# Router logits from the unnormalised rows, an early choice for four tiles, block counts by shift and scan, and a last down product that reads its weights in the ring

## What is computed

```python
def hier_moe(xn, w_rg, b_rg, w_re, b_re, w1, w3, w2):   # xn = rmsnorm(x2) * ffn_norm_g
    lg = xt @ w_rg + b_rg                  # 4 groups, top 1
    le = (xt @ w_re + b_re)[chosen group]  # 8 experts in it, top 2
    gate = pg_top * pe_top / sum(pe_top)
    # rows of one expert lie together, block after block
    ...
    h = silu(xb @ w1[e]) * (xb @ w3[e])    # 1024 -> 512
    y = (h @ w2[e]) * gate                 # 512 -> 1024
    out[token] += y
# then out + x2, and a last rmsnorm with final_norm_g
```

## Time and profile before

| | |
|---|---|
| median of 3 runs | 1295.69 us |
| the profiled execution's own time | 1297.7 us |
| its span, first to last instruction | 1295.9 us |
| mean granted TensorE clock | 0.933 of full speed |
| busy: PE, DVE, ACT, POOL | 1136.1, 516.1, 421.7, 253.7 us |
| weight loads of the experts | 96 of 2048 KB |
| DMA moved | 299.47 MB |

### The profile page before, as it was taken

The page is one execution under the profiler, slowest core; times in us unless marked ns, Lnnn a source line. Parts: engine busy times, 40 slices in busy tenths (PEclk is TensorE's granted clock), DMA queues, the critical chain, the costliest instruction groups (busy, mean ns, idle before and its releaser), DMA issues.

```text
span 1295.9 us, 15806 instructions
## 1 busy us (share of the span) xinstructions
PE 1136.1 (88%) x5178; PEld 699.2 (54%) x5178; DVE 516.1 (40%) x881; ACT 421.7 (33%) x668; POOL 253.7 (20%) x276
## 2 busy tenths in 40 slices
PE   2999999999988977999984899989999879899960
PEld 1788888888856645888873333333333223333320
DVE  3541111112337756755445334433424333424117
ACT  4422222223146555533214124232423332424222
POOL 0011111111107001000000234423434223424220
PEclk9999999999989966999995899989999899999985
DMA  7153331711160001742379399999989999999506
GB/s 292 58 187 114 114 112 50 267 57 49 49 244 1 1 1 52 241 130 87 114 285 415 145 363 393 421 419 419 405 353 378 421 420 419 420 416 405 228 24 279
DMA packets 66591, 299.47 MB, mean 231 GB/s; under 512 B 8672, under 2 KB 8800, under 8 KB 41216
## 3 DMA queue, kind: packets, MB, share of 16 engines
q1 hardware_dynamic: 53488, 264.44, 51.5%
q0 software_dynamic: 13072, 34.63, 6.8%
HBM read 272.29 MB, written 35.91 MB: 238 GB/s over the span
## 4 chain that ended last, share of the span: by engine, by line
PE 62%; DMA 18%; DVE 7%; issue 5%; ACT 5%; SPq 1%; DVEq 0%; ACTq 0%; POOLq 0%; POOL 0%
DMA rawe<-in_w 16%; PE ps L535 12%; PE ps L536 12%; PE ps L537 12%; PE ps L818 11%; PE ps L839 4%; ACT cur L1142 3%; PE ps L634 2%; PE ps L655 2%; PE ps L667 1%; PE ps L808 1%; PE ps L646 1%; PE ps L752 1%; DVE cur13b L1578 1%; DVE att L1291 1%
## 5 line engine op out<-in xcount | busy, mean ns | idle before, releaser
L818 PE MATMUL ps<-cur13a,xT 128*64 128x512 f32 x656 | 163.3, 642 | 37.2 <-DVEq L1580 36.4
L535 PE MATMUL ps<-whi,xTh 128*128 128x512 f32 x480 | 188.2, 392 | 6.2 <-DVE xTl L1228 4.1
L536 PE MATMUL ps<-wlo,xTh 128*128 128x512 f32 x480 | 187.7, 391 | 0.0
L537 PE MATMUL ps<-whi,xTl 128*128 128x512 f32 x480 | 187.6, 391 | 0.0
L839 PE MATMUL ps<-cur,hT 128*64 128x512 f32 x656 | 152.5, 607 | 4.3 <-ACTq L1145 4.3
L1173 DVE TENSOR_TENSOR wlo<-raw,whi 128x2048 fp32r<-128x2048 f32 x27 | 61.7, 2291 | 218.2 <-ACT whi L862 218.0
L818 PE MATMUL ps<-cur13b,xT 128*64 128x512 f32 x656 | 148.6, 592 | 0.0
L1556 DVE COPY xT<-ps 128x512 f32<-128x512 f32 x41 | 28.4, 691 | 296.3 <-PE ps L808 296.3
L818 PEld LDWEIGHTS ps<-cur13a,xT 128*64 128x64 f32 x656 | 53.1, 146 | 118.3 <-issue 116.0
L913 ACT ACTIVATE zst<-ps 128x512 f32<-128x512 f32 x60 | 35.9, 600 | 235.1 <-PE ps L537 235.1
L1142 ACT ACTIVATE cur<-rawe 128x4096 f32 x31 | 112.2, 3620 | 0.1
(11 more groups left out here) (216 smaller groups left out, 1477.3 us busy)
## 6 DMA issues: line engine op xcount, KB each, us to landing
rawe<-in_w SPq DMA_DIRECT2D x96, 2048.0 KB, 17.6
raw<-in_w_in SPq DMA_DIRECT2D x20, 1024.0 KB, 5.8
z_scratch<-zst POOLq DMA_DIRECT2D x60, 256.0 KB, 2.3
gat<-z_scratch SPq DMA_DIRECT2D x12, 512.0 KB, 3.9
xn_scratch<-rrow POOLq DMA_DIRECT2D x6, 1024.0 KB, 4.5
ya<-y_scratch SPq DMA_DIRECT2D x6, 1024.0 KB, 9.9
raw<-in_w_out SPq DMA_DIRECT2D x4, 1024.0 KB, 8.0
xin<-in_x_prompt SPq DMA_DIRECT2D x4, 512.0 KB, 7.8
```

The costliest lines, as they stand in the source:

```text
L535: pe.matmul(out, ah, bh, start=first, stop=False)
L536: pe.matmul(out, ah, bl, start=False, stop=False)
L537: return pe.matmul(out, al, bh, start=False, stop=last)
L818: mm = pe.matmul(ps[0][u * CAP:(u + 1) * CAP, :], xT[:, c, h * CAP:(h + 1) * CAP], cur13[h][:, :, c * 512 + u * 256:c * 512 + u * 256 + 25 ...
```

## The change

1. PE's router columns come from `x2` and no longer from `rrow`, so they wait for `s_x2`. The gain is multiplied into the router weights once, on POOL (a new small load `gcol` on SP, a new semaphore `s_wrg`), and the row's root multiplies the logits in `route_logits`.
2. The logits of tile t-1 stand behind the first quarter of tile t's second half instead of behind the half.
3. `choose` runs for tiles 0 to 3 while the last tile is projected, and for tiles 4 and 5 at the end. PE makes the ranks in two parts to match (`count`): the first ahead of the last tile's logits, the second behind them.
4. The block counts come from a shift by 6 bits and one scan over the 32 experts, instead of the threshold table and five doubling steps. The two picks lie in one tile `A12`, so that one product and one sum serve both. The four steps on the block's expert stand behind the sixth pair of one-hot tables, and PE's product of them behind its ninth table product.
5. POOL's first two gathers take their index straight from `idxt`, and POOL reads the count of blocks behind the first gather instead of ahead of it.
6. The last `down` reads w2 in the ring (`rawe`) and waits for the loads, not for ACT's copy.
7. In the projection's tiles the root takes nine steps (`rsqrt_column`), the first of which nothing waits for. The last norm keeps eleven.

The diff, cut to its core (tile addresses, names of constants and unchanged code that only moved are left out):

```diff
+    A12 = at("A12", D_O + 768, [P, 2, NT, NE])
...
+    wide = at("wide", D_O + 7 * KB, [P, NE])
+    wint = at("wint", D_O + 7 * KB + 128, [P, NE], U32)
+    ends = at("ends", D_O + 7 * KB + 256, [P, NE])
+    zero = at("zero", D_O + 7 * KB + 384, [P, NE])
...
+            sp.dma_start(gcol[:, :], A["ffn_norm_g"][0].rearrange("(p c) -> p c", c=KC)).then_inc(s_rp, 16)
...
-                pe.wait_ge(s_rr, t + 1)
+                pe.wait_ge(s_x2, 2 * t + 2)
...
-                        mm = pe.transpose(ps[j][:, c * P:(c + 1) * P], rrow[t % 2][:, 4 * j + c::KC], ident)
+                        mm = pe.transpose(ps[j][:, c * P:(c + 1) * P], x2[:, t, 4 * j + c::KC], ident)
...
-                    pe.wait_ge(s_rp, 16 * 3)
+                    pe.wait_ge(s_wrg, 1)
...
+                        if t >= 1 and n == 1 and j == 0:
+                            logits(t - 1)
                     mm.then_inc(s_w, 1)
                     if t >= 1 and n == 0:
                         route_columns(t - 1)
-                if t >= 1:
-                    logits(t - 1)
             route_columns(NT - 1)
...
+            def count(a, b, first, last):
+
+                pe.matmul(ps[3][:, a * NE:b * NE], C("tri"), picked[:, a * NE:b * NE],
+                          start=first, stop=False, skip_group_check=True)
+                for u in range(1, NT + 1 - a):
+                    w = min(b, NT + 1 - u)
+                    mm = pe.matmul(ps[3][:, (a + u) * NE:(w + u) * NE], C("ones"), picked[:, a * NE:w * NE],
+                                   start=False, stop=(last and u == NT - a), skip_group_check=True)
+                return mm
+            pe.wait_ge(s_Ab, 1)
+            count(0, NT - 2, True, False)
             logits(NT - 1)
-
-
-            pe.wait_ge(s_Ab, 1)
-            picked = Ab[:, :, :].rearrange("p t e -> p (t e)")
-            pe.matmul(ps[3][:, 0:NT * NE], C("tri"), picked, start=True, stop=False, skip_group_check=True)
-            for u in range(1, NT + 1):
-                mm = pe.matmul(ps[3][:, u * NE:(NT + 1) * NE], C("ones"), picked[:, 0:(NT + 1 - u) * NE],
-                               start=False, stop=(u == NT), skip_group_check=True)
-            mm.then_inc(s_rk, 1)
-
-            pe.wait_ge(s_bc, 1)
-            pe.matmul(ps[5][0:1, 0:P], bcol[:, 0:1], ident, start=True, stop=True).then_inc(s_br, 1)
+            pe.wait_ge(s_Ab, 2)
+            count(NT - 2, NT, False, True).then_inc(s_rk, 1)
 
...
                           start=(q == 0), stop=(q == 2 * NT - 1)).then_inc(s_tbm, 1)
+                if q == NT + 2:
+                    pe.wait_ge(s_bc, 1)
+                    pe.matmul(ps[5][0:1, 0:P], bcol[:, 0:1], ident, start=True, stop=True).then_inc(s_br, 1)
...
-            def down(b):
+            def down(b, last=False):
 
...
-                pe.wait_ge(s_gc, b + 1)
+                if last:
+                    pe.wait_ge(s_w2[1], 16 * NE // 2)
+                else:
+                    pe.wait_ge(s_gc, b + 1)
...
+                            w2 = rawe[:, EW + 4 * PIECE + c:EW + 4 * PIECE + c + 512] if last else cur2[:, c:c + 512]
                             mm = pe.matmul(ps[6][u * CAP:(u + 1) * CAP, :], hT[:, k, h * CAP:(h + 1) * CAP],
-                                           cur2[:, c:c + 512], start=(h == 0 and k == 0), stop=(h == 1 and k == 1))
+                                           w2, start=(h == 0 and k == 0), stop=(h == 1 and k == 1))
...
-            down(nb - 1)
+            down(nb - 1, last=True)
...
-                    act.wait_ge(s_rTm, 2 * (t - 1))
...
+            def rsqrt_column(c, n_mean):
+
+                v, y, a, h = ssq[:, c:c + 1], rstd[:, c:c + 1], rs_a[:, c:c + 1], rs_a[:, 16 + c:17 + c]
+                dve.tensor_scalar(h, v, -0.5 / n_mean, -0.5 * EPS, ALU.mult, ALU.add)
+                link(dve.tensor_scalar(v, v, 1.0 / n_mean, EPS, ALU.mult, ALU.add))
+                link(dve.tensor_scalar(y.bitcast(I32), v.bitcast(I32), -0.5, float(0x5f3759df), ALU.mult, ALU.add))
+                for _ in range(3):
+                    link(dve.scalar_tensor_tensor(out=a, in0=y, scalar=y, in1=h, op0=ALU.mult, op1=ALU.mult))
                     link(dve.scalar_tensor_tensor(out=y, in0=a, scalar=1.5, in1=y, op0=ALU.add, op1=ALU.mult))
...
-                dve.tensor_tensor(lg[:, t, :], ps[2][:, 0:NG + NE], brt[:, :], ALU.add).then_inc(s_rx, 1)
+                dve.scalar_tensor_tensor(out=lg[:, t, :], in0=ps[2][:, 0:NG + NE], scalar=rstd[:, t:t + 1],
+                                         in1=brt[:, :], op0=ALU.mult, op1=ALU.add).then_inc(s_rx, 1)
...
-                pick(A2[:, a:b, :], v[:, 6, :])
-                link(dve.tensor_tensor(Ab[:, a:b, :], A1[:, a:b, :], A2[:, a:b, :], ALU.add))
+                pick(A12[:, 1, a:b, :], v[:, 6, :])
+                dve.tensor_tensor(Ab[:, a:b, :], A12[:, 0, a:b, :], A12[:, 1, a:b, :], ALU.add).then_inc(s_Ab, 1)
...
-            choose(0, NT - 1)
+            for t in range(NT):
+                if t + 1 < NT:
+                    merged_lo(t + 1)
+                else:
+                    choose(0, NT - 2)
...
+                dve.wait_ge(s_sq2, t + 1)
+                rsqrt_column(t, D)
+                if t == 0:
+                    dve.wait_ge(s_rp, 16 * 4)
+                dve.scalar_tensor_tensor(out=rrow[t % 2][:, :], in0=x2[:, t, :], scalar=rstd[:, t:t + 1],
...
             route_logits(NT - 1)
-            choose(NT - 1, NT)
-            dve.sem_inc(s_Ab, 1)
-            link(dve.memset(run[:, :, :], 0.0))
+            choose(NT - 2, NT)
+            dve.memset(zero[:, :], 0.0).then_inc(s_ini, 1)
+            dve.wait_ge(s_ini, 1)
...
-            over = bt[:, 0:NE * (MAXB - 1)].rearrange("p (e j) -> p e j", j=MAXB - 1)
-            link(dve.tensor_tensor(over, cnt.unsqueeze(2).to_broadcast([P, NE, MAXB - 1]),
-                                   C("thr").unsqueeze(1).to_broadcast([P, NE, MAXB - 1]), ALU.is_gt))
-            link(dve.tensor_reduce(nov[:, :], over, AX.X, ALU.add))
-            Z0 = NE // 2
-            link(dve.tensor_copy(run[:, 0, Z0:], nov[:, :]))
-            a, d = 0, 1
-            while d < NE:
-                link(dve.tensor_tensor(run[:, 1 - a, Z0:], run[:, a, Z0:], run[:, a, Z0 - d:Z0 + NE - d], ALU.add))
-                a, d = 1 - a, 2 * d
-            incl = run[:, a, Z0:]
-
-            link(dve.tensor_tensor(first[:, :], incl, nov[:, :], ALU.subtract))
-            link(dve.scalar_tensor_tensor(out=first[:, :], in0=first[:, :], scalar=float(CAP), in1=C("ecap"),
-                                          op0=ALU.mult, op1=ALU.add))
+            link(dve.tensor_scalar(wint[:, :], cnt, float(CAP - 1), None, ALU.add))
+            link(dve.tensor_scalar(wint[:, :], wint[:, :], 6, None, ALU.logical_shift_right))
+            link(dve.tensor_scalar(wide[:, :], wint[:, :], 1.0, float(CAP), ALU.max, ALU.mult))
+            link(dve.tensor_tensor_scan(ends[:, :], wide[:, :], zero[:, :], 0.0, ALU.add, ALU.add))
...
-            for k, Ak in enumerate((A1, A2)):
-                link(dve.tensor_tensor(t2[:, :, :], t1[:, :, :], Ak[:, :, :], ALU.mult))
-                link(dve.tensor_reduce(slotf[:, k, :], t2[:, :, :], AX.X, ALU.add))
+            link(dve.tensor_tensor(t2[:, :, :, :], A12[:, :, :, :],
+                                   t1[:, :, :].unsqueeze(1).to_broadcast([P, 2, NT, NE]), ALU.mult))
+            link(dve.tensor_reduce(slotf[:, :, :], t2[:, :, :, :], AX.X, ALU.add))
...
-            link(dve.tensor_scalar(nbi[:, 1:2], run[0:1, a, Z0 + NE - 1:Z0 + NE], float(NE - 1), None, ALU.add))
-            link(dve.tensor_scalar(nbi[:, 0:1], run[0:1, a, Z0 + NE - 1:Z0 + NE], float(NE), None, ALU.add))
+            for q in range(NT):
+                one_hot(q)
+
+            here = C("tok")[:, 0:1]
+            link(dve.scalar_tensor_tensor(out=last_row[:, :], in0=here.to_broadcast([P, NE]), scalar=float(CAP),
+                                          in1=first[:, :], op0=ALU.mult, op1=ALU.subtract))
+            link(dve.tensor_scalar(t2[:, 0, 0, :], last_row[:, :], 0.0, None, ALU.is_ge))
+            link(dve.tensor_reduce(bcol[:, 2:3], t2[:, 0, 0, :], AX.X, ALU.add))
+            dve.tensor_scalar(bcol[:, 0:1], bcol[:, 2:3], -1.0, None, ALU.add).then_inc(s_bc, 1)
+            for q in range(NT, 2 * NT):
+                one_hot(q)
+            dve.tensor_scalar(nbi[:, 1:2], ends[0:1, NE - 1:NE], 1.0 / CAP, -1.0, ALU.mult, ALU.add)
+            dve.tensor_scalar(nbi[:, 0:1], ends[0:1, NE - 1:NE], 1.0 / CAP, None, ALU.mult)
...
-            link(dve.tensor_copy(served[:, :], ps[5][0:1, 0:NB + 1]))
+            dve.tensor_copy(served[:, :], ps[5][0:1, 0:NB + 1])
             dve.wait_ge(s_tbm, 2 * NT)
-            link(dve.tensor_scalar(idxt[:, :], ps[4][:, 0:NB + 1], -2.0, C("half"), ALU.mult, ALU.add))
-            dve.sem_inc(s_nb, 1)
+            dve.tensor_scalar(idxt[:, :], ps[4][:, 0:NB + 1], -2.0, C("half"), ALU.mult, ALU.add).then_inc(s_nb, 1)
...
```

(30 more changed lines are left out.)

54 lines of the change are left out of this document (22 added, 32 removed).

## The result

The changed kernel takes **1282.28 us** (median of 4 runs, 1277.95 to 1282.88), the kernel before 1296.12 beside it (4 runs, 1295.19 to 1298.73): ratio 0.9883, 95% interval 0.9857 to 0.9909. The forecast was 1283.2 us, 1279.0 to 1289.0. The profiled execution took 1282.33 us for a span of 1280.7.

A forecast was written before the change was run, and what follows sets the result against it. Between the projection's end and the first gather, a 34.9 us chain of small steps was all on the path; at the end, ScalarE's w2 copy. Gains 7.0 + 5.5 = 12.5 took the median from 1295.7 to 1283.2 us, range 1279.0 to 1289.0.

The forecast's parts named there:

- 1 projection's end: Last projection tile: the logits of tile 4 now stand ahead of its last quarter, so it ends 1.7 us later.
- Step 2: Root and router columns of tile 5: the last logits start 1.3 us earlier, at 678.8.
- Step 3: Length of the last logits: 2.75 us, the middle between clocks (1.87 to 3.64); cumulated gain 2.2 us.
- 4 choice: Choice at the end for two tiles instead of one: 0.4 us longer, cumulated gain 1.8 us.
- 5 counts: Counts behind the last choice: six pieces left of 14, 2.15 us less, cumulated gain 3.9 us.
- Step 6: Totals to tables: 3.05 us less in small steps, 1.1 us more in the twelve tables; cumulated gain 5.85 us.
- Step 7: Index release and first gather's issue: 0.15 and 1.0 us saved; cumulated gain 7.0 us, issue at 700.0.
- Step 8: First gather: takes the same 6.7 us (ends 2.8 and 9.0) while the first experts' loads still run.
- Step 9: Blocks' loop: its waits hang on its own copies, so it moves 7.0 us as a whole, load stream included.
- Step 10: Last down product: starts without ScalarE's copy at the high clock; eviction gains 5.5 us, ScalarE late by 1.1 us.
- the rival: Load stream takes the front's gain, or the gather queues behind loads until some 713; 1290.2 us, chance 0.08.
- the blocks start at the low clock: First blocks start and stay at low clock, 4.8 us longer each; four such blocks give 1302.4 us; chance 0.02.

The follow-up runs named there:

- late choice: Changed kernel with the choice for tiles 0 to 4 behind the last scaling, tile 5 at the end, all counts in one piece: 1287.45 us.
- the version with four edits: Changed kernel with earlier bias of tile t-1, block-expert product behind the sixth table product, earlier `xg` clear, no w2 copy in ACT's last block: 1278.76 us.
- held-back gather: Changed kernel with twelve linked clears of `xg` on POOL between the count signal and the first gather: 1289.73 us.
- thresholds twice: Changed kernel with the threshold table and five doubling steps again in place of shift, product and scan, run twice: 1287.74 us and 1289.97 us.
- index copies: Changed kernel with GpSimd's load of the block count and the index copy ahead of the first gathers again: 1283.84 us.
- bias: Changed kernel with the bias of tile t-1 added while ScalarE squares tile t, ahead of the root and scaling: 1279.95 us.
- the two repeats: The changed kernel run twice more, unaltered, beside the kernel before: 1282.71 us and 1283.33 us, ratio 0.9897 each.
- the third trace: Profile of the changed kernel's second repeat, unaltered: median 1283.33 us, ratio 0.9897 to the kernel before.
- the repeated thresholds: Second run of the changed kernel with the threshold table and five doubling steps again: 1289.97 us, beside the changed kernel's 1283.33 us.

## Why the prediction was right

The prediction was right in the waits and overlaps that it named: the gain was made at the front, kept through the loop, and made again at the last down product. Of the sum 12.5 was forecast, and 12.58 and 12.78 are measured from the mark on. That it is so close is in part luck: the logits gave 0.8 more than forecast, the start of the logits and the twelve tables 0.4 less each, and these errors cancel. The profiled execution was forecast at 1285.2 us and took 1282.33; of the 2.9 between them 2.71 arose ahead of the mark, which the prediction did not foresee. Step by step, as it numbered them (gains from the mark, cumulated):

| step | forecast | measured |
|---|---|---|
| 1 projection's end | 1.7 later | 1.9 later |
| 2 last logits start | 1.3 earlier | 0.8 |
| 3 their length; gain | 2.75; 2.2 | 1.96; 2.6 |
| 4 choice; gain | +0.4; 1.8 | +0.5; 2.1 |
| 5 counts; gain | 2.15 less; 3.9 | 2.24 less; 4.4 |
| 6 totals to first table product | 3.05 less | 3.11 less |
| 6 the twelve tables; gain | +1.1; 5.85 | +1.5; 6.0 |
| 7 release and issue; gain | 1.15 less; 7.0 | 1.22 less; 7.2 |
| 8 gather | 6.7 | 6.82 |
| 9 kept through the loop | 7.0 | 6.9 |
| 10 end | 5.5 | 5.6 |

*Step 2* came out 0.4 short, half of it since the projection's end was 0.2 later than forecast. The other half is the root. From the last `x2` to the scaling it is 3.69 us, 0.34 less than before and not 0.5: its squared steps now multiply by a column and take 0.22, where the rows of before had 0.16 for a one-column step.

*Step 3* left the length open between 1.87 and 3.64. The clock was high in every trace in which the early counts stand ahead of the logits (1.95 in all of them), and the late choice shows what the counts are worth to it: the same logits at the same time behind an empty TensorE took 3.60. The middle was the wrong value, and the row that decides it is the sequence ahead (transposes, 14 pieces, logits, with waits of 0.79 and 1.91).

*Step 6* took the scan at the price of one 32-wide step, 0.192, and it took 0.224. For the tables it took the pace of the products of before, 0.448 a pair. The wait in the middle (0.44) and the product of the block's expert (0.52) came near the forecast, but each six pairs took 3.00 instead of 2.69. In the first six VectorE made one pair late: it took 0.70 and 0.54 instead of 0.28 and 0.30, which is worth 0.25 (last section). In the second six the expert's product stands in the middle; in the version with four edits, where it stands between the sixes, each six took 2.81.

*Step 7*: 0.93 us lie between the release by `idxt` and the first gather, which the copy and the load of the count had made longer. The experiment gives 1.2 for both.

*Step 8*: the gather went out while the DMA was 0.99 to 1.01 busy and took 6.82, with the store landed 7.4 ahead of it. It landed at 703.90 while the DMA stayed full until 711.5, so it did not queue behind the loads, which the rival put at some 713. That agrees with the Trainium skill (DMA: Bandwidth & Descriptors, Issuing engines are not separate DMA queues).

*Step 9* (the loop moves as a whole) is the one that the held-back gather tests alone, and it stands: 7.2 at the gather, 7.1 at the eviction. The other runs put a bound on it: that the loop moves as a whole is not a rule. A shift by 2 to 5 us met another clock in the first blocks and in the waits for weights in three runs, and then cost 2 to 4 us more (thresholds twice, late choice); in two more the first block met the high clock sooner, and the end came out 0.7 and 0.9 better than the gather (index copies, bias). The prediction had a part of this as *the blocks start at the low clock*, with 4.8 us a block and 0.02, and 2 us either way in its range; it did not have the waits for weights far behind. In the changed kernel itself the first blocks took 9.24, and 9.16 before, and the longer waits for weights stand at the same blocks in both traces, so it decided nothing. The prediction gave no reason why another start would meet the same clock, and to that extent it was lucky.

*Step 10*: ScalarE was late by 0.93 and not by 1.1. TensorE's product in the ring beside ScalarE's copy of the same bytes took 3.65, and the copy 3.62, each as alone. The Trainium skill's floor of about 0.6 for such a load (DMA: Bandwidth & Descriptors, Latency and other measured facts) is above GpSimd's row of it, 0.48 before and 0.50 in the changed kernel. What the 0.6 would add at the end cannot be told, since the 0.93 has the loop's end in it.

The median fell by 13.8 beside the kernel before, and by 12.6 and 12.9 in the two repeats, around the path's 12.6 to 12.8. The two traces of before reach the mark at 589.0, all twelve others between 581.7 and 588.7, but the kernel before has quick executions too, as told above. Whether the change has a share in the time of the attention stage this study does not show; it stays open.

## What to carry to other kernels

Where a chain of small steps joins two heavy stages, price every step from its own shape's row and follow which engine is released last. Here each step then came out within 0.5 us, but for the one whose clock was left open, which was 0.8 off. Light TensorE work that is due anyway is best put right ahead of a short product on the path: here the early counts paid once by leaving the path and once by the clock of the logits, 1.65 us. And measure from a mark inside the program, behind the last stage that the edit doesn't touch: a stage ahead of it can vary by more than the edit is worth.

## What the runs showed of the hardware

A clear of 128x512 on GpSimd slows VectorE's table steps beside it. The timelines of GpSimd and VectorE of the changed kernel:

```profile
689.66 0.53 POOL L1691 MEMSET xg<- 128x512 f32 x1 [12.48 <-DMA xn_scratch<-rrow]
```

```profile
689.15 0.28 DVE L1535 TENSOR_SCALAR Rt<-cst,sbf 128x128 f32<-128x128 f32 x1
689.56 0.70 DVE L1535 TENSOR_SCALAR Rt<-cst,sbf 128x128 f32<-128x128 f32 x1
690.22 0.27 DVE L1535 TENSOR_SCALAR Rt<-cst,sbf 128x128 f32<-128x128 f32 x1
```

The next step starts 0.66 behind it instead of 0.41, so the clear costs the path 0.25. In the third trace the clear starts at 692.06, and there the two steps from 692.09 on are the long ones, 0.59 and 0.44. In the version with four edits it lies elsewhere, no table step took over 0.31, and the first six products took 0.2 less.

In the blocks' loop behind the first three blocks, the longer waits for weights, 3.8 to 4.3 us in all traces, were followed by 16 products in 5.0 to 6.6 us instead of 3.65. The kernel before and the changed one have four such places each, near 859, 1012, 1044 and 1124 us in the changed kernel; the repeated thresholds have a fifth, near 1194, and that one was worth 4.7 us. Shorter waits, up to 2.6 us, were followed by 3.65, but for two places of the third trace (1.77 and 2.48 us, then 5.35 each). In a kernel that is bound by its loads, what an edit does far behind its place can so be larger than what it does at its place.
